# Down projection by Strassen's seven products, with its token operands made beside gate and up

## The reference

```python
x = x + g1[:, None, :] * mix
h2 = modulate(rms_norm(x, lw['ln2_g']), sh2, sc2)
ff = (jax.nn.silu(h2 @ lw['w_gate']) * (h2 @ lw['w_up'])) @ lw['w_down']
x = x + g2[:, None, :] * ff
```

## Time and profile before

| what | us |
|---|---|
| median of 3 runs (lowest to highest) | 1400.41 (1399.22 to 1403.49) |
| the profiled execution | 1400.21 |
| its span, first to last instruction | 1398.6 |
| PE busy in the span | 1314.4 |
| DVE, ACT, POOL busy | 874.7, 618.8, 596.5 |

### The profile page before, as it was taken

How to read it: one execution, slowest core, us unless ns; L and a number is a source line. 1 busy time by engine, 2 the same in 40 slices (tenths; PEclk the granted TensorE clock), 3 DMA queues, 4 the chain that set the end, 5 groups by cost and what they waited for, 6 DMA issues and landing times.

```text
span 1398.6 us, 24565 instructions
## 1 busy us (share of the span) xinstructions
PE 1314.4 (94%) x9185; PEld 1187.3 (85%) x9185; DVE 874.7 (63%) x1791; ACT 618.8 (44%) x1069; POOL 596.5 (43%) x418
## 2 busy tenths in 40 slices
PE   6889999989579999899999999999999999999998
PEld 4566998887446555699999999999999999999997
DVE  6757889866779844767993344444334466666664
ACT  5536888825967764445533333333333321010002
POOL 0332549992000000255477677767766732121210
PEclk9899999999699998999999999999999999999999
DMA  9622115432101114275412333312332174242203
GB/s 354 235 66 65 47 57 165 157 121 76 31 16 31 52 52 143 75 241 178 126 61 92 106 107 122 111 72 92 122 121 92 61 303 181 92 182 99 114 0 122
DMA packets 117799, 158.65 MB, mean 113 GB/s; under 512 B 16071, under 2 KB 99343, under 8 KB 114608
## 3 DMA queue, kind: packets, MB, share of 16 engines
q1 hardware_dynamic: 117680, 157.08, 32.5%
HBM read 123.99 MB, written 33.10 MB: 112 GB/s over the span
## 4 chain that ended last, share of the span: by engine, by line
PE 69%; DVE 7%; ACT 5%; SPq 5%; POOLq 4%; issue 3%; POOL 3%; DVEq 3%; ACTq 1%; DMA 0%
PE ps L2941 29%; PE ps L2967 6%; PE ps L2966 6%; PE ps L2968 6%; PE ps L2698 2%; PE ps L2686 2%; PE ps L2805 2%; PE ps L2807 2%; PE ps L2806 2%; SPq L600 2%; PE ps L2676 1%; SPq L599 1%; ACT junk L1142 1%; DVEq L2242 1%; POOLq L930 1%
## 5 line engine op out<-in xcount | busy, mean ns | idle before, releaser
L870 POOL TENSOR_TENSOR wL<-wraw,wH 128x1024 fp32r<-128x1024 f32 x36 | 88.5, 2463 | 296.0 <-ACT wH L1135 294.6
L1557 DVE SCALAR_TENSOR_TENSOR xh<-ps,mod,xh 128x344 f32<-128x344 f32 (+1 forms) x264 | 150.3, 571 | 60.4 <-PE ps L2968 60.4
L2941 PE MATMUL ps<-comb,opH 128*128 128x258 f32 x960 | 155.4, 284 | 2.6 <-DVE af L2230 2.6
L2941 PEld LDWEIGHTS ps<-comb,opH 128*128 128x128 f32 x960 | 133.3, 191 | 2.8 <-POOL opL L988 2.8
L988 POOL TENSOR_TENSOR opL<-wsum,opH 128x512 fp32r<-128x512 f32 x80 | 110.2, 1381 | 48.7 <-ACT opH L1436 45.4
L1436 ACT CAST opH<-wsum 128x512 fp32r<-128x512 f32 x80 | 49.6, 622 | 181.3 <-PE ps L2941 98.5
L2941 PE MATMUL ps<-h2H,opL 128*128 128x258 f32 x640 | 129.1, 283 | 0.0
L2941 PE MATMUL ps<-h2L,opH 128*128 128x258 f32 x640 | 129.1, 283 | 0.0
L2941 PE MATMUL ps<-h2H,opH 128*128 128x258 f32 x640 | 128.8, 283 | 0.0
L993 POOL TENSOR_TENSOR dL<-draw,dH 128x1024 fp32r<-128x1024 f32 x22 | 52.5, 2404 | 169.7 <-ACT dH L1507 169.7
L1142 ACT ACTIVATE junk<-score,keyX 128x896 bf16<-128x896 f32 (+2 forms) x96 | 106.0, 1106 | 18.7 <-DVE keyX L1809 13.9
(11 more groups left out here) (484 smaller groups left out, 3851.7 us busy)
## 6 DMA issues: line engine op xcount, KB each, us to landing
adb<-in_ada_w SPq DMA_DIRECT2D x8, 2048.0 KB, 8.3
wraw<-in_w_out SPq DMA_DIRECT2D x24, 512.0 KB, 4.6
draw<-in_w_down SPq DMA_DIRECT2D x22, 512.0 KB, 9.1
raw<-in_w_gate SPq DMA_DIRECT2D x10, 1024.0 KB, 8.5
raw<-in_w_up SPq DMA_DIRECT2D x10, 1024.0 KB, 5.0
ffn_products<-a_odd SPq DMA_DIRECT2D x4, 2064.0 KB, 7.8
ffn_products<-a_even SPq DMA_DIRECT2D x4, 2064.0 KB, 7.4
a_third<-ffn_products SPq DMA_DIRECT2D x3, 2064.0 KB, 8.0
```

The lines of the kernel that those rows point to most:

```text
L870: pool.tensor_tensor(wL[s][:], wraw[s][:], wH[s][:].bitcast(F32), ALU.subtract).then_inc(s_wL, 1)
L1557: return V.scalar_tensor_tensor(out=out, in0=in0, scalar=scalar, in1=in1, op0=op0, op1=op1)
L2941: ins = mm(ps[:, sum_bank(v, p) + h, 0:HC], weight[s][:, k, :], token[:, k, h * HC:(h + 1) * HC], start=begins, stop=ends, skip_group_chec ...
```

## The change

The down projection of the ten pairs is done by Strassen's products as well. Two pairs make a block (`NBLK` = 5): its 512 x 1024 rows of `w_down` and its 512 x 1032 tokens are cut in halves, and seven products P (`DOWN_P` = 1, 6, 7, 5, 2, 4, 3; 35 over all blocks, counted by d) multiply 256 x 512 by 256 x 516. One product has four groups m of 12 matmuls of 258 columns into two banks each, so that four groups fill PSUM. Each p has an accumulator `acc` of 128 x 4 x 516 in SBUF, over all blocks: ScalarE copies the groups of block 0 there (`first_block_out`), VectorE adds those of the others (`down_add`). In the last block VectorE also joins the accumulators (`joined`) and adds them to the residual (`into_x`). The first pair follows in the old form of 24 groups, from HBM (`last_group`, `last_add`).

The weight sums of a block (`dsum`) and the low parts are GpSimd's, the high parts ScalarE's, with four slots for the results. A block's weights are one load of 2 MB into one buffer. The token operands of a block are its seven sums (three of them plain), made in place from the gated results `gf` (three buffers), split into high and low in two staging buffers and stored in HBM; for blocks 0 to 3 this is done beside the gate and up steps of the next block, for block 4 (but its first) beside down's block 0. Down loads each again, 1 MB, into three slots.

The core of the diff:

```diff
-DOWN_SLOTS = 4
+NBLK = FB // 2
+DOWN_P = (1, 6, 7, 5, 2, 4, 3)
+ND = 7 * NBLK
+NG2 = KH * ND
+DOWN_OPS = 4
...
+            def store_input(b, p):
+                n = in_queue(b, p)
+                sp.wait_ge(s_aL, queued(n + 1))
+                sp.dma_start(b_spill[b, p - 1], stg[n % 2][:].bitcast(F32)).then_inc(s_st[n % 2], 16)
...
+            def load_block(b):
+                if b == 0:
+                    sp.wait_ge(s_un, units(item(NST - 1, 6) + 1))
                 else:
...
+                    sp.wait_ge(s_wL, units(len(ITEMS) + 7 * (b - 1) + DOWN_P.index(4) + 1))
+                sp.dma_start(wblk[:], a["w_down"][0][4 * P * b + 2 * P:4 * P * (b + 1) + 2 * P, :].rearrange(
+                    "(f p) n -> p f n", p=P)).then_inc(s_dr[0], 16)
+            def load_input(d):
+                if d < 2:
+                    sp.wait_ge(s_un, units(item(NST - 1, 7) + 1))
+                elif d == 2:
+                    sp.wait_ge(s_un, units(item(NST - 1, 4) + 1))
                 else:
...
+                    sp.wait_ge(s_dn, KH * (d - 2))
+                sp.dma_start(aS[d % A_SLOTS][:].bitcast(F32), b_spill[d // 7, DOWN_P[d % 7] - 1]
+                             ).then_inc(s_ald[d % A_SLOTS], 16)
...
+            load_block(0)
+            all_stored(in_queue(NBLK - 1, 5))
+            for d in range(A_SLOTS):
+                load_input(d)
+            for d in range(ND):
+                if d == 7:
+                    all_stored(in_queue(NBLK - 1, 4) + 1)
+                    for hf in range(2):
+                        sp.dma_start(xh[hf][:], spill[:, KH * hf:KH * (hf + 1), :]).then_inc(s_xr[hf], 16)
+                    for f in range(2):
+                        sp.dma_start(lasta[f][:].bitcast(F32), a_spill[:, f]).then_inc(s_la[f], 16)
+                if d + A_SLOTS < ND:
+                    load_input(d + A_SLOTS)
+                if d < 6:
+                    store_input(NBLK - 1, (5, 2, 3, 6, 7, 4)[d])
+                if d % 7 == 2:
+                    if d // 7 + 1 < NBLK:
+                        load_block(d // 7 + 1)
+                    else:
+                        sp.wait_ge(s_wL, units(len(ITEMS) + 7 * (NBLK - 1) + DOWN_P.index(4) + 1))
+                        for w in range(2):
+                            sp.dma_start(lastw[w][:].rearrange("p f n -> p (f n)"), a["w_down"][0][P * w:P * (w + 1), :]
+                                         ).then_inc(s_dr[1 + w], 16)
...
+            def down_low(d):
+                pool.wait_ge(s_wH, units(len(ITEMS) + d + 1))
+                hi, lo = dO[d % DOWN_OPS]
+                w = down_weight(DOWN_P[d % 7]) if d < ND else lastw[d - ND][:]
+                pool.tensor_tensor(lo[:], w, hi[:].bitcast(F32), ALU.subtract).then_inc(s_wL, 1)
+            def down_sum(p, x, y, op):
+                pool.drain()
+                pool.tensor_tensor(dsum[p][:], x, y, op)
+                pool.drain().then_inc(s_ws, 1)
+            a11, a12 = wblk[:, 0:2, 0:D // 2], wblk[:, 2:4, 0:D // 2]
+            a21, a22 = wblk[:, 0:2, D // 2:], wblk[:, 2:4, D // 2:]
+            for b in range(NBLK):
+                pool.wait_ge(s_dr[0], loaded(b + 1))
+                down_sum(5, a21, a22, ALU.add)
+                down_sum(6, dsum[5][:], a11, ALU.subtract)
+                down_low(7 * b)
+                down_low(7 * b + 1)
+                if b == 0:
+                    pool.wait_ge(s_un, units(item(NST - 1, 4) + 1))
+                down_sum(7, a11, a21, ALU.subtract)
+                down_low(7 * b + 2)
+                down_low(7 * b + 3)
+                down_sum(3, a12, dsum[6][:], ALU.subtract)
+                for i in range(4, 7):
+                    down_low(7 * b + i)
...
+            def input_high(b, p):
+                n = in_queue(b, p)
+                if p in (1, 2, 3):
+                    act.wait_ge(s_af, 3 + 3 * (2 * b + (1 if p == 1 else 2)))
...
+                    act.wait_ge(s_tc, after(4 + 4 * b + (5, 6, 7, 4).index(p) + 1))
+                if n >= 2:
+                    act.wait_ge(s_st[n % 2], stored(n % 2, n // 2))
+                nc.scalar.copy(stg[n % 2][:, :, 0, :], down_input(b, p)).then_inc(s_aH, 1)
...
+                    if u == 1 and b:
+                        input_high(b - 1, 7)
+                    elif u == 2 and b:
+                        input_high(b - 1, 4)
+                    elif u == 3 and v + 1 < NST:
+                        input_high(b, 5)
...
+            def down_high(d):
+                p = DOWN_P[d % 7]
+                if d >= ND:
...
+                elif p in (1, 2, 4):
+                    act.wait_ge(s_dr[0], loaded(d // 7 + 1))
+                else:
+                    act.wait_ge(s_ws, after(2 * NST + 4 * (d // 7) + (5, 6, 7, 3).index(p) + 1))
...
+                else:
+                    act.wait_ge(s_dn, KH * (d - 3))
+                w = down_weight(p) if d < ND else lastw[d - ND][:]
+                nc.scalar.copy(dO[d % DOWN_OPS][0][:], w).then_inc(s_wH, 1)
...
+            def first_block_out(d, m):
+                act.wait_ge(s_dn, KH * d + m + 1)
+                nc.scalar.copy(two(acc[DOWN_P[d]][:, m, :]), ps[:, 2 * m:2 * m + 2, 0:HC]).then_inc(s_dne, 1)
+            down_high(0)
+            down_high(1)
+            for d in range(7):
+                first_block_out(d, 0)
+                first_block_out(d, 1)
+                if d == 0:
+                    down_high(2)
+                first_block_out(d, 2)
+                first_block_out(d, 3)
+                if d == 0:
+                    down_high(3)
+                down_high(d + 4)
+                if d < 6:
+                    input_high(NBLK - 1, (5, 2, 3, 6, 7, 4)[d])
...
+            def input_sum(b, p):
+                x, y = {5: (5, 1), 6: (3, 5), 7: (6, 1), 4: (2, 6)}[p]
+                dve.drain()
+                V.tensor_tensor(down_input(b, p), down_input(b, x), down_input(b, y), ALU.subtract).then_inc(s_tc, 1)
...
+                    if u == 0 and b:
+                        input_low(b - 1, 3)
+                        input_sum(b - 1, 6)
                     dve.drain()
                     third_sum(v)
                     if v + 1 < NST:
                         block22(v)
...
+            def down_add(d, m):
+                p = DOWN_P[d % 7]
+                dve.wait_ge(s_dn, KH * d + m + 1)
+                V.tensor_tensor(two(acc[p][:, m, :]), ps[:, 2 * m:2 * m + 2, 0:HC], two(acc[p][:, m, :]), ALU.add
+                                ).then_inc(s_dne, 1)
+            def joined(x, y):
+                dve.drain()
+                V.tensor_tensor(acc[x][:], acc[x][:], acc[y][:], ALU.add)
+                dve.drain()
...
+            def into_x(p, m):
+                hf, half = {2: (0, 0), 3: (0, 1), 4: (1, 0), 5: (1, 1)}[p]
+                n, w = KH * hf + m, HW if half == 0 else HW - NB
+                xp = xh[hf][:, m, half * HW:half * HW + w]
+                stt(xp, acc[p][:, m, 0:w], mod[:, 40 + n, 0:1], xp, ALU.mult, ALU.add)
...
+                i = d - 7 * (NBLK - 1)
+                for m in range(KH):
+                    down_add(d, m)
+                    if (i, m) == (2, 1):
+                        joined(6, 1)
+                    elif (i, m) == (3, 1):
+                        joined(7, 6)
+                    elif (i, m) == (4, 1):
+                        joined(6, 5)
+                        joined(5, 7)
+                    elif (i, m) == (5, 1):
+                        joined(2, 1)
+                        samples_added(5, 1)
+                        for hf in range(2):
+                            dve.wait_ge(s_xr[hf], loaded(1))
+                    elif (i, m) == (5, 3):
+                        into_x(5, 0)
+                        into_x(5, 1)
+                    elif (i, m) == (6, 0):
+                        into_x(5, 2)
+                        into_x(5, 3)
+                    elif (i, m) == (6, 1):
+                        joined(4, 7)
+                if d % 7 == 6:
+                    dve.drain()
...
+            for m in range(KH):
+                into_x(2, m)
+                into_x(4, m)
+            dve.drain()
+            for q in range(24):
+                last_add(q)
+                if q == 1:
+                    joined(3, 6)
+                    samples_added(3, 0)
+                    dve.drain()
+                elif 2 <= q < 2 + KH:
+                    into_x(3, q - 2)
+                if q % KD == KD - 1:
+                    dve.drain()
...
+            def down_group(d, m):
+                grp = KH * d + m
+                if grp >= 4:
+                    pe.wait_ge(s_dne, grp - 3)
+                else:
+                    pe.wait_ge((s_c12, s_c11, s_c21, s_c12)[grp], after(NST if grp else NST - 1))
...
+                for f in range(2):
+                    cc = slice(m * P, (m + 1) * P)
+                    for weight, part in ((hi, 0), (hi, 1), (lo, 0)):
+                        for h in range(2):
```

(5 more changed lines are left out.)

328 lines of the change are left out of this document (157 added, 171 removed).

## The result

| | before | changed |
|---|---|---|
| median of 7 runs (lowest to highest) | 1400.41 (1395.31 to 1403.62) | 1412.97 (1408.54 to 1416.40) |
| ratio, 95% interval | | 1.0086 (1.0063 to 1.0110) |
| span of the profiled execution | 1398.6 | 1412.8 |
| PE busy in the span | 1314.4 | 1303.7 |

The account below looks back on a forecast made before the run. TensorE, without slack, was taken as the bound: 1376.6 us without waits, plus 1.2 + 2.5 + 10.7 + 9.2 + 9.9 - 1.3 + 3.0, gives 1411.8, say 1411 us. Range 1398 to 1420.

Parts of the forecast that it names:

- What TensorE is spared: Down projection: 247.4 us of matmuls removed, 223.8 added or kept, so TensorE gains 23.6 us.
- Beside gate and up: At step u = 0 of a block, VectorE's added work makes TensorE wait 0.3 us, four times: 1.2 us.
- The second rival: Gate and up lose their cover: GpSimd keeps the port longer, the third sum comes 3.9 us later in four blocks; 1427, 10%.
- Start of down: Before the first down product, TensorE waits for weights, then GpSimd's two sums and low part: 2.5 us (1.5 to 3).
- P5: Down's block 0: ScalarE's cast, waiting for block 1's weights, stands ahead of the copies P5 needs: 6.4 us.
- P7: Down's block 0: ScalarE's high 9, waiting for GpSimd's sum 7, stands ahead of P6's copies and delays P7: 4.3 us.
- P10: Down's block 1: P10's input stands behind 6.3 MB in SyncE's queue, landing 26.4 us in, due at 17.25: 9.2 us.
- The first rival: Requests share the engines, so the queue doesn't hold P10 up and weights come sooner: 1396.6, or 1390 with lower bounds; 20%.
- The tail: Last block and pair: VectorE's continuous joins and additions delay the first transposes 9.9 us (7 to 13), less 1.3 existing waits.
- The clock: Half granted clock behind the waits before P10 and in the tail costs 1.7 us each: 3 us.

Follow-up runs that it names:

- e1_swap: Changed kernel with P10's input asked for just before the 6.3 MB of large loads instead of just behind them: 1408.76 us in one run.
- e6_tail_moved: Changed kernel with large loads spread and ScalarE's casts later, plus accumulator 3's join and additions moved behind the last pair's eighth addition: 1388.35 us, 0.9908 of before.

## Why the prediction was right

The forecast (1411, slower, by waits that give back more than TensorE is spared) held: 1412.97, inside the range. Point by point, against the T of the traces:

- **What TensorE is spared**, 23.6: right. Both pitches came out as read, 119.8 ns for the new matmuls, and the account closes within 1.1 us. The estimate from the figures of the Trainium skill (TensorE: Matmul & The Clock Gate, Back-to-back issue gap), by which TensorE alone would lose 7, does not fit these matmuls.
- **Beside gate and up**, 1.2: measured 0. VectorE's load rose by 14.7 points, 13 were forecast. The second rival (1427) is out.
- **Start of down**, 2.5: 1.31. GpSimd's two sums and low part ran from 1132.11 to 1140.2, 8.1 us, with less lost to VectorE than I had put in, and the weights landed 7.0 us ahead of TensorE's need (1131.95, 1138.9) in place of 6.4; just below the range of 1.5 to 3.
- **P5**, 6.4: 7.58. The mechanism was as described (released by a ScalarE copy behind a cast that waited 10.07 us for the weights). The request went at P2's end + 4.7 (5.1 forecast); the transfer took 12.1 for 10.1, because two more transfers of 1 MB that I left out were still ahead in the queue, a store asked for at 1156.02 (landed 1164.16) and P5's own input, asked for at 1157.84 (landed 1166.60). I also left out that P6's input comes behind the weights; here the gap before P5 covered that.
- **P7**, 4.3: 2.62. From the landing to P7 it took 18.7 (15.5 to 20.4 forecast); P7 was due later because P5's products ran at half clock.
- **P10**, 9.2: 7.91. The input landed 26.9 us into block 1, 26.4 was forecast; the half clock behind P7 had made P10 due 1.6 later. The first rival fell by the landings, 7.7, 12.2, 14.2 and 18.3 us in order of request, and by e1_swap.
- **The tail**, 9.9 less 1.3: 7.8 less 0.8. The joins took 2.31 as forecast. The place was wrong: the sum had TensorE run to the first transposes and wait there, but it waited at the ninth group for a bank. That made the lower T of e6_tail_moved possible.
- **The clock**, 3: 6.5. This is the step that failed. I let half clock follow two gaps; it followed four, P7's of only 2.62 too, and the spells lasted 3 to 5 us. It did not lengthen the total by the full 3.5, since part of it filled waits that would have been there: the four waits up to P10 come to 19.4 for 22.4 forecast.

The sum was +11.6 against the old execution; T gives +10.5, and the medians differ by 12.6. That the median and the sum agree so well is partly luck: waits too large by some 6 us stood against a clock term too small by 3.5.

What stays open: the 1.3 to 1.6 us before P0, which hang on GpSimd's chain behind a landing, and the 2.0 to 3.0 before P6, which hang on its input behind block 1's weights, were not attacked. To let that input go ahead of the weights was not tried, nor were two weight buffers for GpSimd, nor was the difference between last pieces of 8.0 and 9.0 to 9.8 us explained.

## What to carry to other kernels

When an algorithm saves work on the bound engine, list for each in-order queue what now stands ahead of the first thing that engine needs: here a prefetch of 6.3 MB nobody needed for 150 us ahead of an input due in 10, and a cast that waited for a load ahead of the copies that free PSUM. Both took a few lines to move and turned 0.9% slower into 0.7% faster. Waits in a row cover each other, so an edit that removes one may show less than its gap until the next is gone as well: the gap before P10 grew when that before P5 went, and a wait of P6 came to light that P5's had covered. And count half clock behind each gap of some 2 us or more, as a cost that may come.
